# Expert weights loaded in two half-height transfers: a two-layer encoder with a mixture of experts on one core

## The chip, the core and the metric

The program runs on one NeuronCore of a Trainium2 chip. The metric is the device time of one execution in microseconds (us); the time of a kernel is the median of its runs.

## What is computed

The reference is an encoder of two layers on 256 tokens of width 1024, all in float32. Each layer has a mixer (a long convolution and a differential attention) and a feed-forward part. The feed-forward part of layer 0 is dense; that of layer 1 is a mixture of eight experts, of which each token takes two. Cut to what matters here:

```
def swiglu(x, w_gate, w_up, w_down):
    return (jax.nn.silu(x @ w_gate) * (x @ w_up)) @ w_down

def moe_ffn(x, w_router, w_gate, w_up, w_down):
    logits = (xt @ w_router).astype(F32)
    top_val, top_idx = lax.top_k(logits, TOP_K)
    ...
    def run(args):
        xb, e = args
        return swiglu(xb, w_gate[e], w_up[e], w_down[e])
    ...
```

D_MODEL is 1024, D_FF 2752, N_EXPERTS 8, TOP_K 2. The three float32 matrices of one expert are 33.8 MB, and the kernel reads all eight experts.

## The kernel before

All weights are streamed from HBM in slabs. A slab is at most 128 partitions x 2048 float32 (1 MiB, 8 KB in each partition). SyncE issues the loads in the order in which TensorE will use them, and waits before each until its place in SBUF is free. The stages are the mixer of layer 0, the dense feed-forward part, the mixer of layer 1, and the mixture of experts, here the expert stage. In the first three stages the slabs go to six `raw` places, and ScalarE and VectorE split each into two parts (`w_hi`, `w_lo`) for TensorE. These loads are issued by `put` and are of no concern to the change.

In the expert stage TensorE reads the slabs as they land. Eight blocks follow one another, one for each expert. A block has 34 slabs: 33 are loaded by the lines at L792 to L796 (30 of 1 MiB, two of 768 KB, one of 512 KB), and the last, `last_rows`, by four transfers of 16 partitions x 4 KB (L785). The 33 go to the twelve places of `ring`; the first twenty places of the stage also use eight other buffers that have come free by then (`h_slot`, the two halves of `filters`, `xv_slot`, `tmp_dft_slot`, two `gate_slots`, `hT_lo_slot`). So SyncE starts to load the experts while the mixer of layer 1 still runs: six of them (the places of `h`, `filters0`, `filters1`, `xv`, 0 and 1) ahead of the router.

Two things order the loads. `slot_free` makes SyncE wait on `slab_used`, which TensorE counts up after the last matmul that reads a slab. Each place has a semaphore `raw_loaded`, to which a landed transfer adds 16, and TensorE's `loaded` waits for the value that `loaded_by_place` gives. The twelve ring places enter the stage with the count that the `raw` loads left on the first six of them.

On TensorE a block is six chunks of `gate_up_moe` (L2121 in blocks with room for 64 tokens, L2126 with 96) and the `down` steps between them (L2136 and L2143, or L2157). There is also a code path for further blocks, in a hardware loop, for experts with more tokens than their room.

Of the kernel before, what the change touches and what calls it, by code (L numbers as in the profile page):

```python
# [32 lines left out]
P = 128  # L33
# [9 lines left out]
NE, TOPK = 8, 2  # L43
# [3 lines left out]
RAW_SLOTS, SPLIT_SLOTS = 6, 3  # L47
# [25 lines left out]
RING = 2 * RAW_SLOTS  # L73
# [7 lines left out]
MOE_PLACES = MOE_SLABS - 1  # L81
SKIPPED = 3
# [10 lines left out]
PLACE = {("mix", 0): 0, ("ffn", 0): MIX_SLABS, ("mix", 1): MIX_SLABS + FFN_PLACES, ("ffn", 1): 2 * MIX_SLABS + FFN_PLACES}  # L93
# [7 lines left out]
def raw_slot(stage, p):  # L101
    return raw_place(stage, p) % RAW_SLOTS
# [7 lines left out]
def width_of(stage, p):  # L110

    return FFN_WIDTHS[p % FFN_SLABS] if stage[0] == "ffn" else SLAB
# [5 lines left out]
MOE_AT = [P * sum(MOE_WIDTHS[:p]) for p in range(34)] + [3 * FF * D]  # L118
# [15 lines left out]
def slot_of(place):  # L134

    return FIRST_TURN[place] if place < len(FIRST_TURN) else RING_ORDER[(place - len(FIRST_TURN)) % RING]


def loaded_by_place(place):

    slot, turn = slot_of(place), 0 if place < len(FIRST_TURN) else 1 + (place - len(FIRST_TURN)) // RING
    return 16 * (turn + 1) + (16 * (PLACE["ffn", 1] // RAW_SLOTS) if slot in range(RAW_SLOTS) else 0)


def is_late(b, p):
# [4 lines left out]
def moe_place(b, p):  # L150

    return MOE_PLACES * b + p + (SKIPPED if is_late(b, p) else 0)
# [124 lines left out]
def trunk(nc, x_in, slabs, par_d, lamv_d, hid_d, wf3_d, hyb_d, nffn_d, wr_d,  # L277
# [21 lines left out]
    def sem(name):  # L299
        if name not in semaphores:  # L300
            semaphores[name] = ctx.enter_context(nc.semaphore(name))
        return semaphores[name]
# [118 lines left out]
    def bank(step, i):  # L421
        return PS[BANKS[step][i]]
# [9 lines left out]
    def weight(b, p):  # L432

        slot = slot_of(moe_place(b, p))
        return EXTRA_AT[slot] if slot in EXTRA else SLOTS[:, slot, :]
# [44 lines left out]
    def wait_drained(eng, layer, step, i):  # L480

        eng.wait_ge(*drain_of(layer, step, i))
# [235 lines left out]
    def _(sp):  # L718
# [10 lines left out]
        slot = raw_slot(("mix", 0), 0)  # L729
# [5 lines left out]
        for layer in range(DEPTH):  # L735
            stage, first = ("mix", layer), FIRST["mix", layer]
            for p in range(0 if layer else 1, MIX_SLABS - layer):
                slot = raw_slot(stage, p)
                put(slot, RAW[:, slot, :], slabs["mix"][layer, p], raw_place(stage, p))

            if layer == 0:
                for p in (0, 2):
                    slot, at = raw_slot(("ffn", 0), p), slice(SLAB_AT[p], SLAB_AT[p + 2])
                    put(slot, RAW[:, slot, :].rearrange("p (h n) -> p h n", h=2),
                        slabs["dense"][0, at].rearrange("(h p n) -> p h n", h=2, p=P), raw_place(("ffn", 0), p))
                for p in range(4, FFN_SLABS):
                    slot, at, width = raw_slot(("ffn", 0), p), slice(SLAB_AT[p], SLAB_AT[p + 1]), width_of(("ffn", 0), p)
# [4 lines left out]
        def slot_free(b, at, p):  # L752

            place = moe_place(at, p)
            slot = slot_of(place)
            if place >= len(FIRST_TURN):
                blocks, slab = freed_by(at, p)
                sp.wait_ge(slab_used, MOE_SLABS * b + (MOE_SLABS * blocks + slab + 1 + first))
            elif slot == "h":
                wait_filled(sp, 1, "sc3", 1)  # L760
            elif slot in ("filters0", "filters1"):
                sp.wait_ge(event("ys_ready", 1), 2)
            elif slot == "xv":
                wait_filled(sp, 1, "yT", 1)
            elif slot == "tmp_dft":
                sp.wait_ge(event("merged", 1), 4)
            elif slot == "gates0":
                wait_filled(sp, 1, "mTb", 1)
            elif slot == "hT_lo":
                wait_filled(sp, 1, "rt", 1)  # L770
            elif slot in range(RAW_SLOTS):
                sp.wait_ge(lo_ready, slab_at(PLACE["ffn", 1] + slot - RAW_SLOTS) + 1)
            elif slot in range(RING):
                sp.wait_ge(slab_used, first - SPLIT_SLOTS + 1 + (RING_ORDER.index(slot) - RAW_SLOTS) // 2)

        def load_slab(e, b, at, p):

            if p == MOE_SLABS - 1:
                if at == 0:
                    sp.wait_ge(sem("last_rows_zeroed"), 1)  # L780
                else:
                    sp.wait_ge(slab_used, MOE_SLABS * b + first)
                rows = (TAIL - P) // 4
                for q in range(4):
                    sp.dma_start(R["last_rows"][QUARTER * q:QUARTER * q + rows, :],  # L785
                                 slabs["moe"][e, MOE_AT[p] + q * rows * D:MOE_AT[p] + (q + 1) * rows * D]
                                 .rearrange("o (r n) -> (o r) n", n=D)).then_inc(last_rows_loaded, 16)
                return
            to, width = weight(at, p), MOE_WIDTHS[p]
            loaded = raw_loaded[slot_of(moe_place(at, p))]  # L790
            slot_free(b, at, p)
            pieces = 2 if at == NE and p in REJOINED else 1  # L792
            for i in range(pieces):
                cols = slice(i * width // pieces, (i + 1) * width // pieces)
                sp.dma_start(to[:, cols],  # L795
                             slabs["moe"][e, MOE_AT[p]:MOE_AT[p + 1]].rearrange("o (p n) -> p (o n)", p=P)[:, cols]).then_inc(loaded, 16)  # L796

        def load_block(e, b):

# [16 lines left out]
        with sp.If(nb > NE):  # L816
            with sp.Fori(NE, nb) as b:
                e = sp.value_load(R["nbe"][0:1, bass.ds(b, 1)], min_val=0, max_val=NE - 1)
# [917 lines left out]
    def _(pe):  # L1736
# [87 lines left out]
        for layer in range(DEPTH):  # L1824
# [141 lines left out]
            if layer == 1:  # L1966
# [4 lines left out]
                for kd in range(KD):  # L1971
# [6 lines left out]
                    for tb in range(TB):  # L1978
                        tok = slice(tb * P, (tb + 1) * P)
                        both = R["wr_parts"][:, kd, :, :].rearrange("p a e -> p (a e)")  # L1980
                        to = bank("rt", tb)
# [17 lines left out]
            tbs, rows = TB, P  # L1999
# [74 lines left out]
            def pick_tokens(b, room):  # L2074

                pe.wait_ge(psel_ready, b + 1)
                cols = 32 if room == CAP else 64
                for kd in range(KD):
                    for tb in range(TB):
                        for q in range(0, P, cols):  # L2080
                            ins = mm(picked_to(kd)[q:q + cols, 0:room], X[:, tb, kd * P + q:kd * P + q + cols], R["psel"][:, tb, 0:room],
                                     start=tb == 0, stop=tb == TB - 1)
                    if kd % 4 == 3:
                        ins.then_inc(picked, 1)

            def dense_block():

                n0 = first

                def slot(p):  # L2090
                    return (first + p) % SPLIT_SLOTS
                for part in range(4):
                    gate_up(n0 + part, slot(part), 2 * part, 2, CHUNK, 0, 0, "fht")
                    if part == 0:
                        turn_h(0, 2)
                        turn_h(0, 3)
                for c in range(1, NCH + 1):
                    p, parity, width = 3 * c + 1, c % 2, CHUNK if c < NCH else TAIL
                    gate_up(n0 + p, slot(p), 0, 4, width, c, parity)
                    turn_act(c - 1, 1 - parity)  # L2100
                    gate_up(n0 + p + 1, slot(p + 1), 4, 4, width, c, parity)
                    down(n0 + p + 2, slot(p + 2), c - 1, c == 1)
                turn_act(NCH, 0)
                down(n0 + 34, slot(34), NCH, False, tiles=((0, P),))
                down_last(n0 + 35, slot(35), NCH)
# [91 lines left out]
            def turn_spread(b):  # L2197

                pe.wait_ge(sem("spread_ready"), b - (NE - 2))
                rows = CAP if is_heavy(b) else LCAP  # L2200
                for tb in range(TB):
                    ins = nc.tensor.transpose(PS[0][0:rows, tb * P:(tb + 1) * P], R["spread_sum"][:, tb, 0:rows], IDENT[:, :])
                ins.then_inc(sem("spread_turned"), 1)
# [14 lines left out]
            if layer == 0:  # L2218
                dense_block()
            else:  # L2220
                wait_drained(pe, 1, "pos", 0)
                pick_tokens(0, LCAP)
                for b in range(NE - 1):
                    moe_block(b)
                moe_block(NE - 1, None, lambda: turn_spread(NE - 1))
                spread(NE - 1)
                pe.wait_ge(sem("blocks_known"), 1)
                nb = pe.value_load(R["nbi"][0:1, 0:1], min_val=NE, max_val=NBLK)
                with pe.If(nb > NE):
                    with pe.Fori(NE, nb) as b:  # L2230
                        pe.wait_ge(sem("combined"), 4 * b + 4)
                        pick_tokens(b, CAP)
                        turns = pe.snap(16 * ((MOE_PLACES + SKIPPED) // RING) * b - 16 * ((MOE_PLACES + SKIPPED) // RING) * NE)
                        moe_block(b, turns, lambda: turn_spread(b))
                        spread(b)

# [135 lines left out]
```

## Time and profile before

| | us |
|---|---|
| median of 3 runs | 1295.62 (1294.94 to 1297.51) |
| the profiled execution | 1296.07 |
| its span | 1294.3 |
| TensorE busy, matmuls | 1217.1 (94%) |
| VectorE, ScalarE, GpSimd busy | 608.0, 337.8, 45.1 |
| chain that ended last | TensorE 71%, DMA 12%, VectorE 5% of the span |

The span is the time from the first to the last instruction; some 1.8 us of the execution lie outside it. A window of the trace gives, for a stretch, each engine's busy time, the clock that TensorE was granted (1.00 is full), the mean busy share of the core's 16 DMA engines and the bytes that they moved. A packet is put down whole to the moment that it starts, so a share can pass 1 in a short window.

### The profile page before, as it was taken

The page shows a single profiled execution, that of the slowest core. Times are in us where ns is not written, and L with a number is a line of the kernel's source. Part 1 is how long each engine was busy: PE and PEld are TensorE (multiplying, and loading weights), DVE is VectorE, ACT ScalarE, POOL GpSimd, SP SyncE. Part 2 cuts the span into 40 slices and gives each one's busy share as a digit, 9 for nine tenths or more (in the row PEclk, how much of TensorE's full clock was granted, in tenths as well). Part 3 has the DMA queues.
Part 4 walks back from the last instruction along what each step waited for, and adds up shares of the span by engine and source line. Part 5 has one row for each costly group of instructions (what it writes and reads, how often), then busy time and mean ns, then how long its engine had stood idle before and what let it go on. Part 6 is the DMA issues. An engine that isn't in the chain of part 4 may idle for free.

```text
span 1294.3 us, 24431 instructions
## 1 busy us (share of the span) xinstructions
PE 1217.1 (94%) x10627; PEld 775.8 (60%) x10627; DVE 608.0 (47%) x1078; ACT 337.8 (26%) x519; POOL 45.1 (3%) x56
## 2 busy tenths in 40 slices
PE   6999999999999999999999999889999988898966
PEld 5787678888887887778644553245645522454212
DVE  6888987655544988987362113211111032111223
ACT  4444554643443444464300000000000000000000
POOL 0011010100000011010000000000000000000010
PEclk9999999999999999999999999999999999999999
DMA  9434433755543344446799999999999999999994
GB/s 349 154 136 157 163 127 137 273 179 190 187 147 130 135 159 163 163 171 254 330 379 397 420 395 421 420 396 420 389 419 420 388 422 402 403 420 387 421 420 178
DMA packets 55876, 376.13 MB, mean 291 GB/s; under 512 B 6706, under 2 KB 7298, under 8 KB 13780
## 3 DMA queue, kind: packets, MB, share of 16 engines
q1 hardware_dynamic: 54690, 370.17, 72.8%
q0 software_dynamic: 1072, 4.33, 1.1%
q8 instruction: 86, 1.41, 0.4%
q14 instruction: 26, 0.21, 0.1%
q10 hardware_dynamic: 2, 0.00, 0.0%
HBM read 371.07 MB, written 3.41 MB: 289 GB/s over the span
## 4 chain that ended last, share of the span: by engine, by line
PE 71%; DMA 12%; DVE 5%; SPq 2%; issue 1%; ACT 1%; POOL 0%; DVEq 0%; ACTq 0%
PE bank L2126 17%; DMA ring<-in_moe 12%; PE bank L1741 8%; PE bank L1742 8%; PE bank L2136 6%; PE bank L2121 6%; PE bank L2042 4%; PE bank L1791 4%; PE bank L2019 3%; PE bank L2143 3%; PE bank L2157 2%; DVE ys L1196 1%; SPq L795 1%; PE bank L1886 1%; PE bank L1754 1%
## 5 line engine op out<-in xcount | busy, mean ns | idle before, releaser
L2126 PE MATMUL bank<-ring,hT_block 128*32 128x256 f32 (+1 forms) x4608 | 230.3, 357 | 4.9 <-issue 4.7
L1207 DVE TENSOR_TENSOR w_lo<-raw,w_hi 128x2048 fp32r<-128x2048 f32 (+2 forms) x92 | 201.4, 2201 | 52.5 <-ACT w_hi L907 52.3
L1741 PE MATMUL bank<-w_hi,hT_hi 128*128 128x512 f32 (+1 forms) x528 | 209.3, 396 | 2.4 <-DVE hT_lo L1196 1.6
L1615 DVE TENSOR_TENSOR act_moe<-silu_moe,bank 128x256 f32<-128x256 f32 (+1 forms) x40 | 19.5, 488 | 398.4 <-ACT silu_moe L1141 398.4
L1742 PE MATMUL bank<-w_hi,hT_lo 128*128 128x512 f32 (+1 forms) x528 | 205.1, 388 | 0.0
L2126 PEld LDWEIGHTS bank<-ring,hT_block 128*32 128x32 f32 x4608 | 143.7, 110 | 95.8 <-issue 14.2
L907 ACT ACTIVATE w_hi<-raw 128x2048 fp32r<-128x2048 f32 (+2 forms) x92 | 169.1, 1848 | 88.5 <-PE bank L1791 42.7
L2121 PE MATMUL bank<-ring,hT_block 128*64 128x512 f32 (+1 forms) x704 | 144.4, 550 | 22.8 <-DMA ring<-in_moe 22.8
L1141 ACT ACTIVATE silu_moe<-bank 128x256 f32<-128x256 f32 (+3 forms) x48 | 19.7, 410 | 544.6 <-PE bank L2126 303.6
L2121 PEld LDWEIGHTS bank<-ring,hT_block 128*64 128x64 f32 x704 | 47.9, 136 | 119.4 <-issue 64.7
L1741 PEld LDWEIGHTS bank<-w_hi,hT_hi 128*128 128x128 f32 x528 | 99.2, 188 | 24.9 <-issue 4.5
L1742 PEld LDWEIGHTS bank<-w_hi,hT_lo 128*128 128x128 f32 x528 | 99.2, 188 | 20.2 <-issue 1.0
L2157 PE MATMUL bank<-ring,act_T 128*64 128x512 f32 x336 | 80.9, 610 | 19.8 <-DMA ring<-in_moe 19.2
L2136 PE MATMUL bank<-ring,act_T 128*32 128x512 f32 x672 | 90.2, 593 | 1.2 <-issue 1.2
L1791 PE MATMUL bank<-w_lo,hT_hi 128*128 128x512 f32 x352 | 87.9, 392 | 0.5 <-DVE w_lo L1207 0.3
L1791 PEld LDWEIGHTS bank<-w_lo,hT_hi 128*128 128x128 f32 x352 | 65.5, 188 | 15.5 <-DVE w_lo L1207 1.7
L2157 PEld LDWEIGHTS bank<-ring,act_T 128*64 128x64 f32 x336 | 23.4, 138 | 71.1 <-issue 51.5
L2143 PE MATMUL bank<-ring,act_T 128*32 128x512 f32 x336 | 50.6, 592 | 0.0
L1623 DVE STREAM_TRANSPOSE act_T<-act_moe 32x128 f32<-32x128 f32 x160 | 48.4, 303 | 2.6
L2136 PEld LDWEIGHTS bank<-ring,act_T 128*32 128x32 f32 x672 | 25.5, 110 | 40.0 <-issue 36.9
L1741 PE MATMUL bank<-hT_hi,w_hi 128*128 128x256 f32 x192 | 47.1, 286 | 0.0
L1742 PE MATMUL bank<-hT_lo,w_hi 128*128 128x256 f32 x192 | 46.5, 283 | 0.0
(282 smaller groups left out, 1200.7 us busy)
## 6 DMA issues: line engine op xcount, KB each, us to landing
ring<-in_moe SPq DMA_DIRECT2D x232, 1024.0 KB, 23.4
raw<-in_mix SPq DMA_DIRECT2D x56, 1024.0 KB, 4.8
raw<-in_dense SPq DMA_DIRECT2D x30, 1024.0 KB, 4.7
ring<-in_moe SPq DMA_DIRECT2D x16, 768.0 KB, 26.1
ring<-in_moe SPq DMA_DIRECT2D x8, 512.0 KB, 24.0
filters<-in_moe SPq DMA_DIRECT2D x2, 1024.0 KB, 9.9
gate_slots<-in_moe SPq DMA_DIRECT2D x2, 1024.0 KB, 11.0
last_rows<-in_moe SPq DMA_DIRECT2D x32, 64.0 KB, 15.2
```

Of the source, the lines that this page charges most:

```text
L907: nc.scalar.activation(HI[:, split_slot, 0:width], RAW[:, raw_slot, half:half + width], ACT.Copy)\
L1207: vec.tensor_tensor(LO[:, split_slot, 0:width], RAW[:, raw_slot, half:half + width], HI[:, split_slot, 0:width].bitcast(F32), ALU.subtract ...
L1623: ins = vec.transpose(R["act_T"][to:to + QUARTER, c % 2, 0:tiles, QUARTER * t:QUARTER * t + QUARTER], act_tile(c)[frm:frm + QUARTER, i * t ...
L1741: mm(out_, left[0], right[0], start=start, stop=False)
L1742: mm(out_, left[1], right[1], start=False, stop=False)
L1791: ins = mm(bank(step, tb)[:, :], HTH[:, kd, tok], w_lo, start=False, stop=sp_)
L2042: ins = mm(PS[4 + 2 * tb + half][0:rows, :], left[0:h, k, tok], right[0:h, s, at:at + 512], start=first and k == 0, stop=last and k == 1)
L2121: ins = mm(x_banks(c)[64 * half:64 * half + 64, 0, 0:2 * width], tokens[:, kd, 0:LCAP], at[:, (4 * k + 2 * half) * width:(4 * k + 2 * half ...
L2126: ins = mm(x_banks(c)[QUARTER * q:QUARTER * q + QUARTER, t, 0:width], tokens[:, kd, QUARTER * t:QUARTER * t + QUARTER], at[:, (4 * k + q) ...
L2136: ins = mm(Y_BANKS[half][q:q + 32, :], left[:, k, 32 * t:32 * t + 32], rights[k][:, half * 512:half * 512 + 512], start=start and k == 0, ...
L2143: ins = mm(Y_BANKS[1 - k][q:q + 32, :], left[:, k, 64:96], rights[k][:, half * 512:half * 512 + 512], start=start, stop=stop)
L2157: ins = mm(Y_BANKS[half][64 * half:64 * half + 64, :], left[:, k, 0:LCAP], rights[k][:, half * 512:half * 512 + 512], start=start and k == ...
```

## The change

Each of the 33 large loads of a block is issued as two transfers, one that writes partitions 0 to 63 and one that writes partitions 64 to 127, each of the full width of the slab. Both add 16 to the same semaphore, so the value that TensorE waits for rises by 32 for each use of a place. `last_rows`, the results that go out to `slot_y`, and the loads of the other stages are as before.

```diff
@@ def loaded_by_place(place):
-    return 16 * (turn + 1) + (16 * (PLACE["ffn", 1] // RAW_SLOTS) if slot in range(RAW_SLOTS) else 0)
+    return 32 * (turn + 1) + (16 * (PLACE["ffn", 1] // RAW_SLOTS) if slot in range(RAW_SLOTS) else 0)
@@ def load_slab(e, b, at, p):
             for i in range(pieces):
                 cols = slice(i * width // pieces, (i + 1) * width // pieces)
-                sp.dma_start(to[:, cols],
-                             slabs["moe"][e, MOE_AT[p]:MOE_AT[p + 1]].rearrange("o (p n) -> p (o n)", p=P)[:, cols]).then_inc(loaded, 16)
+                for rows in (slice(0, P // 2), slice(P // 2, P)):
+                    sp.dma_start(to[rows, cols],
+                                 slabs["moe"][e, MOE_AT[p]:MOE_AT[p + 1]].rearrange("o (p n) -> p (o n)", p=P)[rows, cols]).then_inc(loaded, 16)
@@ the loop of further blocks, on TensorE
-                        turns = pe.snap(16 * ((MOE_PLACES + SKIPPED) // RING) * b - 16 * ((MOE_PLACES + SKIPPED) // RING) * NE)
+                        turns = pe.snap(32 * ((MOE_PLACES + SKIPPED) // RING) * b - 32 * ((MOE_PLACES + SKIPPED) // RING) * NE)
```

This is what SyncE issues before, from the first expert slab to the end of the first block (`raw<-in_mix` is the mixer's last slab):

```order
L795 DMA h_slot<-in_moe 128x2048
L795 DMA filters<-in_moe 128x2048 x2
L795 DMA xv_slot<-in_moe 128x2048
L723 DMA raw<-in_mix 128x2048
L795 DMA ring<-in_moe 128x2048 x2
L795 DMA tmp_dft_slot<-in_moe 128x2048
L795 DMA ring<-in_moe 128x2048 x4
L795 DMA gate_slots<-in_moe 128x2048 x2
L795 DMA ring<-in_moe 128x2048 x6
L795 DMA hT_lo_slot<-in_moe 128x2048
```

And the same place in the changed kernel:

```order
L796 DMA h_slot<-in_moe 64x2048 x2
L796 DMA filters<-in_moe 64x2048 x4
L796 DMA xv_slot<-in_moe 64x2048 x2
L723 DMA raw<-in_mix 128x2048
L796 DMA ring<-in_moe 64x2048 x4
L796 DMA tmp_dft_slot<-in_moe 64x2048 x2
L796 DMA ring<-in_moe 64x2048 x8
L796 DMA gate_slots<-in_moe 64x2048 x4
L796 DMA ring<-in_moe 64x2048 x12
L796 DMA hT_lo_slot<-in_moe 64x2048 x2
```

The order of the slabs is the same; each stands there as two neighbours with half the partitions. From the second block on the expert's number is read at run time, and before each transfer stands one more instruction (ISA). This is SyncE at the start of the second block, in the changed kernel:

```order
L785 DMA last_rows<-in_moe 16x1024 x4
L814 TENSOR_LOAD nbe
L814 ISA x2
L796 ISA
L796 DMA ring<-in_moe 64x2048
L796 ISA
L796 DMA ring<-in_moe 64x2048
```

Before, an ISA and one transfer of 128x2048 stood there for each slab; now there are two such pairs. The other engines' instructions are the same, but for the values that TensorE waits for.

## Rows read from the trace of the kernel before

**Rows 1.** The page: GB/s moved, in 40 slices of the span.

```profile
GB/s 349 154 136 157 163 127 137 273 179 190 187 147 130 135 159 163 163 171 254 330 379 397 420 395 421 420 396 420 389 419 420 388 422 402 403 420 387 421 420 178
```

**Rows 2.** Windows of the expert stage: window, us, engines' busy time, PEclk, DMA share, GB/s.

```profile
604.00:622.00 18.00, 18.00 (x89) 15.12 (x88) 8.86 (x11) 7.93 (x14) 0.95 (x1) 1.00 0.96 389
622.00:640.00 18.00, 16.69 (x153) 13.62 (x153) 7.61 (x33) 6.81 (x16) 1.31 (x4) 1.00 1.01 422
640.00:647.00 7.00, 7.00 (x35) 2.77 (x32) 1.26 (x4) 0.38 (x1) 0.00 (x0) 1.00 0.04 16
647.00:1272.00 625.00, 577.14 (x7390) 268.97 (x7388) 128.66 (x409) 32.49 (x85) 3.92 (x4) 1.00 1.01 406
```

**Rows 3.** Waits of TensorE after 640 us: total us, times, longest.

```profile
PE bank L2121 <- DMA ring<-in_moe: 22.8, 31, 1.8
PE bank L2157 <- DMA ring<-in_moe: 19.2, 21, 2.2
```

**Rows 4.** DMA issues of the page: count, KB each, median us from issue to landing.

```profile
ring<-in_moe SPq DMA_DIRECT2D x232, 1024.0 KB, 23.4
...
last_rows<-in_moe SPq DMA_DIRECT2D x32, 64.0 KB, 15.2
```

**Rows 5.** Timeline of SyncE's queue, 570 to 604 us: start, us, what was issued.

```profile
570.70 0.43 SPq L795 DMA_DIRECT2D h_slot<-in_moe  x1
...
581.58 0.33 SPq L723 DMA_DIRECT2D raw<-in_mix  x1
583.89 4.92 SPq L795 DMA_DIRECT2D ring<-in_moe  x2
603.70 0.33 SPq L795 DMA_DIRECT2D tmp_dft_slot<-in_moe  x1
```

**Rows 6.** Timeline of SyncE's queue at the start: a load of 64 partitions x 8 KB.

```profile
2.89 0.48 SPq L707 DMA_DIRECT2D wf<-in_wf  x1
```

**Rows 7.** Windows while that load ran.

```profile
6.50:7.00 0.50, 0.50 (x2) 0.22 (x2) 0.00 (x0) 0.50 (x3) 0.00 (x0) 1.00 0.92 197
7.00:7.50 0.50, 0.50 (x2) 0.00 (x0) 0.00 (x0) 0.50 (x3) 0.00 (x0) 1.00 0.94 197
7.50:8.00 0.50, 0.05 (x1) 0.00 (x0) 0.32 (x1) 0.50 (x3) 0.00 (x0) 1.00 1.04 213
8.00:8.50 0.50, 0.00 (x0) 0.00 (x0) 0.47 (x2) 0.48 (x3) 0.11 (x1) 1.00 1.14 238
```

**Rows 8.** Issues of 512 KB in the DMA list: `raw` 128 partitions, `wf` 64 partitions.

```profile
raw<-in_dense SPq DMA_DIRECT2D x1, 512.0 KB, 3.1
wf<-in_wf POOLq DMA_DIRECT2D x1, 512.0 KB, 4.7
```

**Rows 9.** Windows in which the first four `last_rows` transfers ran.

```profile
680.00:681.00 1.00, 1.00 (x8) 0.32 (x6) 0.00 (x0) 0.00 (x0) 0.00 (x0) 1.00 1.09 246
681.00:682.00 1.00, 1.00 (x8) 0.40 (x6) 0.00 (x0) 0.00 (x0) 0.00 (x0) 1.00 0.80 115
682.00:683.00 1.00, 1.00 (x6) 0.29 (x4) 0.00 (x0) 0.00 (x0) 0.00 (x0) 1.00 0.88 205
```

**Rows 10.** Windows at the end of the stream.

```profile
1264.00:1265.00 1.00, 0.87 (x6) 0.00 (x0) 0.00 (x0) 0.00 (x0) 0.00 (x0) 1.00 1.04 430
1272.00:1273.00 1.00, 1.00 (x6) 0.17 (x4) 0.90 (x2) 0.00 (x0) 0.00 (x0) 1.00 0.45 188
1280.00:1281.00 1.00, 0.99 (x6) 0.42 (x8) 0.00 (x0) 0.00 (x0) 0.00 (x0) 1.00 0.12 49
```

**Rows 11.** The chain that ended last, after 1255 us: start, us, what.

```profile
1253.74 26.23 DMA ring<-in_moe
```

**Rows 12.** ScalarE's splits of the mixer's last slabs, 575 to 640 us.

```profile
L907 ACT ACTIVATE w_hi<-raw x6: 1915/1920/1922, 579.6 to 607.4; 128x2048 fp32r<-128x2048 f32 x6
```

**Rows 13.** Windows with a granted clock under 1.00.

```profile
852.00:854.00 2.00, 2.00 (x8) 0.38 (x6) 0.00 (x0) 0.00 (x0) 0.00 (x0) 0.50 0.97 397
854.00:856.00 2.00, 2.00 (x12) 0.47 (x12) 0.02 (x1) 0.03 (x1) 0.00 (x0) 0.93 1.06 442
```

## The prediction

> **What bounds the kernel now.** I read the page's row of rates first. Up to about 600 us the DMA engines move 127 to 330 GB/s after the first slice; from there to the end it is 387 to 422 [rows 1]. So the only part that the change touches is also the only one in which memory traffic is dense. The windows of that stage show both sides nearly full: from 647 to 1272 us TensorE is busy 577 of 625 us, and the 16 DMA engines have a busy share of 1.01 at 406 GB/s; the best stretch, 622 to 640 us, has 422 [rows 2], which I take as the full rate. The waits tell which of the two leads. TensorE stood still for transfers 22.8 and 19.2 us in blocks with room for 64 tokens [rows 3], and in the others hardly at all. A slab lands 23.4 us after its issue [rows 4]; at 422 GB/s 1 MiB takes 2.48 us, so some nine slabs are queued. The stage is balanced, and has nothing with which to pay for a slower stream: nearly all that the transfers lose, the end loses.
>
> **The change part by part.** The bytes are the same. Of 264 large loads, six are issued before 603.70 us [rows 5], while there is slack; the other 258 (234 of 1 MiB, 16 of 768 KB, 8 of 512 KB) are 250 MiB, 262.1 MB, and from 603.70 us the queue is never empty in the changed kernel if it slows down.
>
> *Issuing.* 258 more issues. One takes 0.33 to 0.43 us of SyncE's queue [rows 5], 0.48 at the start [rows 6]. Two per slab are under 1 us, against 2.48 us for moving it: hidden, cost 0. Uncovered, it would be 258 x 0.43 = 111 us, but the nine slabs in the queue cover it. TensorE's waits keep their number and place.
>
> *Moving half a slab.* The trace before has no stream of 64-partition loads, but it has one such load: `wf`, 64 partitions x 8 KB, the packet size of the slabs, issued at 2.89 us behind others [rows 6]. While it ran, 6.5 to 8.5 us, the engines moved 197, 197, 213 and 238 GB/s, 211 on average, at a busy share of about 1 [rows 7]. The reader is to see the two columns together: all 16 engines are at work, and they move half of what they move for 128 partitions. So it isn't that half of the engines do the work; each works at half speed, as two of them would that write through one entry to SBUF. Its second copy, on GpSimd's queue, agrees: 4.7 us to landing against 3.1 for 512 KB over 128 partitions [rows 8], though others ran beside it.
>
> *Two neighbours in the queue.* Do an upper and a lower half fill each other's gap? The four `last_rows` loads are the nearest row: 16 partitions each, two in the lower half and two in the upper, issued in a row. In 680 to 683 us the engines moved 246, 115 and 205 GB/s at shares of 0.80 to 1.09 [rows 9]: 0.57 MB where 1.27 would pass, so 1.66 us lost, and 2.3 us for four loads that need 0.62 at the full rate. They ran nearly one after another, each at its own narrow rate. If the halves do the same, the rate is 211.
>
> The Trainium skill speaks against this change too: SBUF — State Buffer, section "Can I just issue two DMAs to hit both halves?", answers no, with 6% gained by two concurrent transfers at partitions 0 and 64 over one; its section on the port swizzle has 196 GB/s for partitions 0 to 63 at 1 MiB. By the page the rate would be 208 GB/s, and the sum below 1920 us as an estimate. The trace's 211 agrees with the 196; that neighbours don't help, rows 9 show for narrow loads only.
>
> *What speaks for more than 211.* The 16 engines don't march in step for long. All loads had been issued when, at 1264 us, the share was 1.04; it was 0.45 at 1272 and still 0.12 at 1280 [rows 10], so the first and the last engine finish some 16 us apart. Half a slab at the full rate takes 1.24 us. Two engines that share an entry and are a whole half-slab apart don't meet at all: one is in the lower half while the other is in the upper. If such distances are spread evenly, half of the bytes meet and half do not, and the rate is 2 / (1/211 + 1/422) = 281 GB/s. The stream starts in step, though (the queue runs dry before 603.70), engines that both wait for one entry can't drift apart by their own speed, and a slab counts as landed only when the slowest pair has it. I choose a point a quarter of the way from 211 to 281 in time per byte: 1 / (0.75/211 + 0.25/281) = 225 GB/s. This is the number of the prediction with the least behind it; both ends stay in the range.
>
> *The sum.* Start of the dense stream 603.7. The halves: 262.1 MB / 225 = 1165. `last_rows` 8 x 2.3 = 18. The results to `slot_y`, seven blocks, 2.4 MB at the full rate: 6. The lag of the last engine, 16. From the last landing (1253.74 + 26.23 = 1280.0 [rows 11]) to the end of the span 14.3. Together 1823 us of span; with the 1.8 outside it 1825, and the profiled execution lies 0.45 over the median, which changes nothing here. The same sum with 422 GB/s and the 7 us of an empty queue at 640 [rows 2] gives 1288 for the kernel before, 8 short of its 1296; the rest is that the fast engines waited and TensorE held the ring. The added semaphore writes I set at 0.
>
> *What waits ahead.* The mixer's last slab is issued behind four expert slabs, at 581.58 us [rows 5]. These end at about 570.7 + 4.2 MB / 225 = 589, and it lands near 593. ScalarE starts its last split at 607.4 us [rows 12], so 14 us cover it. The six slabs before the router land by 604 plus a few us, TensorE begins the experts at about 640; from place 12 or so it waits for each slab, about 4.7 us apart, of which it computes 2.5.
>
> **The rivals.**
>
> *The halves stay in step throughout:* 211 GB/s, 262.1 / 211 = 1242, end at 1902 us. For it: rows 7 and 9, both of short stretches. Against it: rows 10. Chance 0.20.
>
> *The engines drift apart further than I think:* 281 to 400 GB/s, 933 to 655 us in place of 1165, end between 1593 and 1315. For it rows 10. Against it that contention itself holds them together. Chance 0.15.
>
> *Nothing happens:* each pair settles a half-slab apart and stays there, since nothing then disturbs it; or the entry isn't what limits `wf`. The rate is 422 as before, TensorE and the waits are the same, 1296 us. Rows 9 speak against it, in their short stretch. Chance 0.12.
>
> *Faster:* the same full rate, and in addition the work of a slow entry is shared between two engines, which takes away up to half of the 16 us by which the last engine lags: 1288 us. It decides only if the rate stays above some 415 GB/s. Nothing in the rows shows what slows an engine. Chance 0.05.
>
> *TensorE's clock falls:* with 577 us of work in some 1200 it idles half of the time. At a granted 0.50 (1.2 GHz of 2.4) it started 8 matmuls in 2 us where it started 12 in the next 2 us, at 0.93 [rows 13]. All its expert work at the lower level would be about 1154 us, nearly the stream's own time, and what doesn't overlap comes on top: 1940 to 2000 us. Against it: through 48 us of short idle times between 647 and 1272 us the mean clock stayed at 1.00 [rows 2]. Chance 0.06.
>
> **How the numbers follow.** My forecast, a rate between 213 and 281 GB/s, ends between 1593 and 1892 us: chance 0.42, the value 1825. With steps of 0.20, 0.15, 0.12, 0.05 and 0.06 for the others that makes 1. The range goes from 1400 (a rate of 354) to 1940: it leaves out no change and faster, the smaller part of the further drift, and the upper part of the clock's case, together about 2 in 10. The likeliest case's own range is 1593 to 1902. Slower by over 0.2%, which is about what a measurement of this kernel can tell from no change: 0.20 + 0.15 + 0.42 + 0.06 = 0.83. Same 0.12, faster 0.05.
>
> **What would show it.** In windows after 650 us a DMA share of about 1 at 210 to 280 GB/s; if the share is 1 and the rate 420, the halves do not meet. If the share is near 0.5, the halves are served by half of the engines each, and my reading of rows 7 is wrong. TensorE's waits for `ring` should sum to some 500 to 600 us, in both kinds of block; SyncE should wait for free places as before, since the ring is still full of loads under way. If the rate rises from block to block, the engines drift apart; if it is flat at 211, they don't. If the rows before 570 us differ, something other than the halves has changed. The number would be wrong most easily by my quarter of the way: each 10 GB/s there is about 50 us.

## The result, and the profile after

| | before | changed |
|---|---|---|
| median, us | 1295.28 (1293.46 to 1297.51) | 1641.61 (1621.79 to 1647.79) |
| profiled execution, us | 1296.07 | 1635.77 |
| span, us | 1294.3 | 1633.9 |

The change makes the kernel slower by a quarter: the ratio of the times is 1.257, 95% interval 1.248 to 1.267. This ratio is taken from the two faster of the four executions; the ratio of the medians is 1.267. The change also makes the time less steady: its four executions lie within 1.6% of one another, where those of the kernel before lie within 0.3%.

These are windows of the changed kernel, with the columns of [rows 2].

```profile
604.00:622.00 18.00, 18.00 (x89) 15.09 (x88) 8.85 (x11) 7.92 (x14) 0.95 (x1) 1.00 1.02 219
650.00:750.00 100.00, 66.50 (x502) 24.31 (x502) 23.67 (x107) 3.41 (x10) 0.00 (x0) 0.90 1.02 230
850.00:950.00 100.00, 59.59 (x464) 17.91 (x464) 13.69 (x41) 2.62 (x6) 0.00 (x0) 0.95 1.02 270
950.00:1050.00 100.00, 68.10 (x856) 30.09 (x860) 13.30 (x43) 3.62 (x10) 0.00 (x0) 0.98 1.02 285
1150.00:1250.00 100.00, 69.61 (x1107) 32.93 (x1103) 6.91 (x19) 2.89 (x8) 0.00 (x0) 0.97 1.02 260
1250.00:1350.00 100.00, 63.17 (x424) 19.41 (x413) 16.75 (x52) 4.04 (x11) 0.00 (x0) 0.96 1.02 295
647.00:1612.00 965.00, 652.26 (x7390) 263.10 (x7388) 129.88 (x409) 32.41 (x85) 3.93 (x4) 0.95 1.01 270
```

Read the last two columns together, as in [rows 7]. The 16 DMA engines are busy all the time (1.02), at 219 GB/s when the dense stream begins, where [rows 2] had 389 and 422. Then the rate climbs, to 230, 270 and 285, falls back to 260, and comes to 295. TensorE is busy 652 of 965 us.

The trace also holds the time of each packet, which no view prints. In 622 to 640 us, 923 of 925 packets of 8 KB took under 350 ns in the kernel before (median 309). In the changed kernel each of the 484 took 525 ns or more, with a median of 612: every packet takes twice as long. In 950 to 1050 us the median is 461 ns; 260 of 3145 took under 350, and 2314 took 350 to 550.

The waits of TensorE after 640 us, which answer to [rows 3]:

```profile
PE bank L2122 <- DMA ring<-in_moe: 119.4, 70, 4.0
PE bank L2127 <- DMA ring<-in_moe: 89.7, 83, 2.4
PE bank L2158 <- DMA ring<-in_moe: 50.2, 27, 3.1
PE bank L2137 <- DMA ring<-in_moe: 34.6, 26, 3.2
```

Now both kinds of block wait, 294 us in these four groups. The issue row that answers to [rows 4]:

```profile
ring<-in_moe SPq DMA_DIRECT2D x464, 512.0 KB, 31.9
```

And the end of the chain, which answers to [rows 11]:

```profile
1589.41 30.55 DMA ring<-in_moe
...
1620.01 1.94 PE bank L2158 x8
```

The last landing is at 1619.96 us, and 13.9 us follow it, as 14.3 did before.

### The profile page after: what moved, and what is told of

It is laid out like the page before. It is cut to its first block, busy times and chain, and to the rows that moved or that the text cites. A ratio compares the mean times of both kernels' runs of the same rounds, so it can differ in the third digit from the quotient of the medians.

```text
span 1633.9 us, 25157 instructions
## 1 busy us (share of the span) xinstructions
PE 1292.8 (79%) x10627; PEld 770.7 (47%) x10627; DVE 607.8 (37%) x1078; ACT 337.8 (21%) x519; POOL 45.0 (3%) x56
## 4 chain that ended last, share of the span: by engine, by line
SPq 42%; PE 29%; DMA 14%; issue 4%; DVE 4%; ACT 0%; POOL 0%; DVEq 0%; ACTq 0%
SPq L796 39%; DMA ring<-in_moe 10%; PE bank L1742 7%; PE bank L1743 6%; PE bank L2043 4%; PE bank L1792 3%; DMA hT_lo_slot<-in_moe 3%; PE bank L2020 2%; DMA last_rows<-in_moe 2%; SPq L785 1%; SPq L805 1%; DVE ys L1197 1%; PE bank L1887 1%; PE bank L1755 1%; PE bank L1787 1%
## 5 line engine op out<-in xcount | busy, mean ns | idle before, releaser
L2127 PE MATMUL bank<-ring,hT_block 128*32 128x256 f32 (+1 forms) x4608 | 245.3, 362 | 98.7 <-DMA ring<-in_moe 89.7
L2122 PE MATMUL bank<-ring,hT_block 128*64 128x512 f32 (+1 forms) x704 | 168.0, 606 | 119.7 <-DMA ring<-in_moe 119.4
L2127 PEld LDWEIGHTS bank<-ring,hT_block 128*32 128x32 f32 x4608 | 136.9, 111 | 217.0 <-DMA ring<-in_moe 132.6
L2158 PE MATMUL bank<-ring,act_T 128*64 128x512 f32 x336 | 96.0, 700 | 54.4 <-DMA ring<-in_moe 50.2
## 6 DMA issues: line engine op xcount, KB each, us to landing
ring<-in_moe SPq DMA_DIRECT2D x464, 512.0 KB, 31.9
```

Source lines behind the costliest of these rows:

```text
L2122: ins = mm(x_banks(c)[64 * half:64 * half + 64, 0, 0:2 * width], tokens[:, kd, 0:LCAP], at[:, (4 * k + 2 * half) * width:(4 * k + 2 * half ...
L2127: ins = mm(x_banks(c)[QUARTER * q:QUARTER * q + QUARTER, t, 0:width], tokens[:, kd, QUARTER * t:QUARTER * t + QUARTER], at[:, (4 * k + q) ...
L2158: ins = mm(Y_BANKS[half][64 * half:64 * half + 64, :], left[:, k, 0:LCAP], rights[k][:, half * 512:half * 512 + 512], start=start and k == ...
```

## The experiments

Theory A is the prediction's: a transfer that writes only partitions 0 to 63, or only 64 to 127, reaches half of the entries to SBUF, so that the 16 engines, all at work, share them; the cost falls as the engines drift apart (the distances between them in the stream change). The first rival is that the number or the size of the transfers costs. All edits but that of `e11_one_last` are made to the changed kernel. Medians of 4 or more runs unless said otherwise; the kernel before, beside them on the same chip, had 1294.6 to 1295.6 us.

| run | edit | us |
|---|---|---|
| e1_columns | halves by columns | 1310.60 |
| e12_even_odd | even and odd partitions | 1295.56 |
| e4_turned | lower, upper, upper, lower | 1787.47 |
| e7_quads | quarters, lower and upper by turns | 1632.80 |
| e8_quads_grouped | quarters, two lower, two upper | 1715.45 |
| e2_lead4, e3_lead8 | 4 or 8 small transfers on an empty queue | 1643.28, 1652.68 |
| e5_mid4, e6_mid8 | 4 or 8 small transfers, 8 rows, in a full queue | 1618.98, 1639.55 |
| e9_engines4 | 4 small transfers, 4 rows | 1650.53 |
| e10_engine1 | 4 small transfers, 1 row | 1610.18 (one run) |
| e11_one_last | kernel before, last rows in one wide transfer | 1284.42 |

### Is it the number of transfers?

```diff
-                for rows in (slice(0, P // 2), slice(P // 2, P)):
-                    sp.dma_start(to[rows, cols],
...
+                for j in range(2):
+                    cols = slice((2 * i + j) * width // (2 * pieces), (2 * i + j + 1) * width // (2 * pieces))
+                    sp.dma_start(to[:, cols],
...
```

> Each slab goes as two transfers again, but cut by columns: all 128 partitions and half of the row (4 KB in place of 8 KB) in each. Number of transfers, semaphore values and bytes are those of the changed kernel. Theory A (a 64-partition transfer reaches only half of the entries to SBUF, two engines at each): full rate, 405 to 422 GB/s in the expert stage, 1290 to 1305 us. Theory B (twice as many transfers in the queue are what costs: SyncE's issues fill 39% of the chain of the changed kernel): the rate stays at 220 to 300 GB/s and the time at 1600 to 1660 us.

1310.60 us, a ratio to the kernel before of 1.012 (1.011 to 1.014), and some 6 us above the expected range. Two windows:

```profile
622.00:640.00 18.00, 16.70 (x152) 13.76 (x152) 7.61 (x33) 6.80 (x16) 1.31 (x4) 1.00 1.03 409
1050.00:1150.00 100.00, 83.53 (x822) 32.92 (x822) 23.47 (x77) 4.77 (x13) 0.00 (x0) 1.00 1.02 400
```

409 GB/s where [rows 2] has 422, at a full share: the engines are as busy and move 3% less, which goes with the 4 KB packets. The same number of transfers with shorter packets thus costs 16 of the 346 us. The number costs nothing, as the run with even and odd partitions shows.

### Is it 64 partitions, or one side of SBUF?

```diff
-                for rows in (slice(0, P // 2), slice(P // 2, P)):
+                for rows in (slice(0, P, 2), slice(1, P, 2)):
```

> The changed kernel with the two transfers of a slab taken as the even and the odd partitions, in place of the lower and the upper half. Both are 64 partitions with 8 KB each, and each reaches both halves of SBUF. Theory A as it first stood (what counts is how many of the entries to SBUF a transfer reaches as a whole): full rate, 1290 to 1315 us. Theory A as the small transfers have left it (what counts is which engines are at the same entry at the same time, with groups of engines that share entries): each engine now writes two packets to one half and two to the other; engines in step still meet, but half the distance parts them: the stream starts at 220 to 300 GB/s and climbs faster than in the changed kernel, 1400 to 1600 us. Rival (64 partitions in a transfer cost the same wherever they are): 1610 to 1660 us.

1295.56 us over ten runs; the ratio to the kernel before is 1.0007 (0.9998 to 1.0017), no change. Three windows:

```profile
605.00:622.00 17.00, 17.00 (x85) 14.22 (x84) 8.76 (x11) 7.71 (x13) 0.95 (x1) 1.00 0.92 370
622.00:640.00 18.00, 16.70 (x152) 14.11 (x152) 7.71 (x34) 7.02 (x18) 1.31 (x4) 1.00 1.01 422
647.00:1272.00 625.00, 581.56 (x7408) 273.07 (x7406) 131.03 (x413) 32.42 (x85) 3.93 (x4) 0.99 1.01 406
```

The last two are the rates of [rows 2], 422 and 406. Of its packets of 8 KB in 622 to 640 us, 921 of 925 took under 350 ns. It has the number of transfers, packets of 8 KB, semaphores and issues of the changed kernel, so the whole loss hangs on which 64 partitions a transfer holds. Theory A as it first stood forecast this; my amended form, in which even and odd partitions would still meet, did not. But the first form, which counts the entries of one transfer alone, says nothing of the climb and of the effect of order that follow.

One thing moves with the partitions in every edit here: the rows in HBM that the transfer reads. No run separates the two. Against HBM as the cause speaks only this: the small transfers further down read rows of the first expert slab and write nothing to SBUF, and nearly all their packets took 309 to 312 ns in the midst of halves whose packets took some 600.

### Does the cost depend on how long an engine stays on one side?

```diff
@@ e4_turned
-                for rows in (slice(0, P // 2), slice(P // 2, P)):
+                for rows in ((slice(0, P // 2), slice(P // 2, P)), (slice(P // 2, P), slice(0, P // 2)))[moe_place(at, p) % 2]:
```

> The changed kernel with the order of the two halves turned in every second slab: lower, upper, upper, lower. Each engine then stays in the same half of SBUF for two transfers in a row. Theory A with drift: the engines of a pair must be twice as far apart to miss each other, so the rate climbs later from 211 to 220 GB/s and the time is longer than 1642, by some 30 to 120 us. Rival (the cost is per transfer, or on the side of HBM): no difference, 1620 to 1650 us.

1787.47 us (1758.87 to 1799.12), 146 more than the changed kernel: the sign as expected, the size above the 30 to 120. Its fastest execution is 111 us above the slowest of the changed kernel. Its windows:

```profile
650.00:750.00 100.00, 68.00 (x428) 23.33 (x428) 24.25 (x109) 3.41 (x10) 0.00 (x0) 0.83 1.02 217
1250.00:1350.00 100.00, 64.82 (x1011) 32.07 (x1004) 4.94 (x12) 2.69 (x8) 0.00 (x0) 0.97 1.02 232
1650.00:1750.00 100.00, 59.24 (x194) 14.07 (x193) 20.83 (x55) 1.92 (x5) 3.92 (x4) 0.83 1.00 275
```

The rate climbs here too, but at 1250 us it is 232 where the changed kernel has 295. Bytes, transfers and packets are the same; only the order differs, and with it an engine's stay on a side, which is twice as long.

The second pair of kernels cuts each half by columns too, and differs in order alone (semaphores count 64 per slab):

```diff
@@ e7_quads
-                for rows in (slice(0, P // 2), slice(P // 2, P)):
+                for rows, part in ((lower, 0), (upper, 0), (lower, 1), (upper, 1)):
+                    cols = slice((2 * i + part) * width // (2 * pieces), (2 * i + part + 1) * width // (2 * pieces))
@@ e8_quads_grouped
+                for rows, part in ((lower, 0), (lower, 1), (upper, 0), (upper, 1)):
```

> Each slab goes as four transfers of 64 partitions and half of the columns (4 KB rows), in the order lower, upper, lower, upper. Semaphore values are 64 per slab. An engine now stays in one half of SBUF for 16 KB, half as long as in the changed kernel. Theory A with drift: half the distance is enough to miss each other, so the rate leaves 211 to 220 GB/s sooner: 1540 to 1620 us (the 4 KB packets cost some 1.2% of the rate, as the columns run showed). Rival (cost by number of transfers or by packet): well above 1650.

> The same four transfers per slab in the order lower, lower, upper, upper. Number, size and packets are those of the run before; only the order differs. An engine stays in one half of SBUF for 32 KB, as in the changed kernel. Theory A with drift: 1620 to 1680 us, and 50 to 120 us above the alternating order. Rival (number and size of transfers alone matter): the same time as the alternating order.

1632.80 (1620.70 to 1643.07) and 1715.45 us (1659.49 to 1769.00): 83 us apart by their medians, inside the 50 to 120, though each is above its own range, by 13 and 35 us. The executions of the grouped order scatter over 110 us. The fastest of them is 16 us above the slowest with alternating order, so the sign is sure and the size is not. One window of each, from the slowest execution of each, first the alternating order:

```profile
950.00:1050.00 100.00, 67.67 (x716) 26.84 (x710) 11.83 (x39) 2.63 (x7) 0.00 (x0) 0.91 1.04 261
```

and the grouped one:

```profile
950.00:1050.00 100.00, 59.67 (x448) 20.80 (x452) 10.26 (x35) 2.65 (x8) 0.00 (x0) 0.85 1.04 228
```

Two pairs of kernels that differ in order alone say the same: a shorter stay on one side costs less. It is what drifting engines would give, but the stay isn't all. The grouped order has the stay of the changed kernel, 32 KB, and is 74 us slower by the medians. The alternating order has half of it and is only 9 us faster. Cutting finer cost 16 us where all 128 partitions were written; here it seems to cost more, and no run shows why.

### Can the engines be set apart by hand?

Small transfers from HBM to an unused HBM buffer, ahead of the seventh slab (e2, e3) or the fifteenth (the others), were to hold back some engines:

```diff
+        def lead():
+
+            for i in range(LEAD):
+                rows = slabs["moe"][0, 0:P * SLAB].rearrange("(p n) -> p n", p=P)[0:32:4, :]
+                sp.dma_start(aside[:, 2 * i * SLAB:(2 * i + 1) * SLAB], rows).then_inc(sem("led"), 16)
...
+            if at == 0 and p == 6:
+                lead()
```

`e5_mid4` and `e6_mid8` have `p == 14`; `e9_engines4` has rows `[0:16:4, :]`, `e10_engine1` the one row `[0:1, 0:SLAB - 1]`.

> The changed kernel with four small transfers ahead of the dense stream (before the seventh expert slab): 8 rows of 8 KB each, from HBM to an unused HBM buffer, which should occupy eight of the sixteen DMA engines for four packets, as long as half a slab takes at the full rate. Theory A with drift (two engines share an entry only while both are in the same half, and start in step): the pairs now start half a slab apart, so the stream starts at 380 to 420 GB/s where the changed kernel has 218 to 230, and falls as the engines drift; if they keep their distance the time is near 1300, if they lose it within some hundred us 1450 to 1600. Rival (the half rate has nothing to do with when the engines meet): 218 to 230 GB/s at first, 1620 to 1650 us.

> The same with eight of the small transfers, so that the distance is two half-slabs: both engines of a pair are in the same half again. Theory A with drift: 215 to 240 GB/s at first, as in the changed kernel, 1600 to 1650 us. If the small transfers help by something else than the distance, this kernel gains as much as the one with four.

1643.28 us (1589.14 to 1685.21) and 1652.68 (1640.83 to 1690.84). The first had 227 GB/s in 605 to 622 us, where theory A wanted 380 to 420, so both came out as the rival said. They are weak evidence, though: the queue was empty, SyncE issued the small transfers 0.67 us apart while one packet takes 0.31, and the first half-slab was issued when they were done.

> The changed kernel with four small transfers of 8 rows x 8 KB (HBM to an unused HBM buffer) ahead of the fifteenth expert slab. Ahead of the seventh slab the queue was empty, so that SyncE's own issue times spaced the small transfers out and eight engines were not held back behind the others. Here some ten transfers stand in the queue, and the four are worked off back to back. Theory A with drift: from the moment they are worked off (about 640 to 670 us) the pairs are half a slab apart, and the rate in the windows of 10 us behind it rises from 220 to 350 to 420 GB/s, and falls back in the next hundred us or so as the engines drift; the total is 20 to 200 us below 1642. Rival (the distance within a pair doesn't matter, or the pairs are not one of the first eight engines with one of the last eight): 220 to 230 GB/s as in the changed kernel.

> The same place with eight small transfers: the distance is two half-slabs and the engines of a pair are in the same half again. Theory A with drift: 210 to 240 GB/s behind them, apart from the some 3 us in which the small transfers themselves run, and a total of 1610 to 1660 us. If it rises as in the run with four, it isn't the distance.

1618.98 us (1612.16 to 1647.78) and 1639.55 (1613.73 to 1660.55). The windows of the second, before, during and after its small transfers:

```profile
635.00:645.00 10.00, 8.99 (x98) 4.90 (x98) 0.86 (x4) 1.60 (x6) 0.00 (x0) 1.00 1.03 227
645.00:655.00 10.00, 10.00 (x48) 4.00 (x46) 7.97 (x35) 0.77 (x2) 0.00 (x0) 1.00 1.01 251
655.00:665.00 10.00, 10.00 (x50) 4.05 (x48) 5.56 (x26) 0.38 (x1) 0.00 (x0) 1.00 1.00 224
```

The small transfers are 0.52 MB, which alone would add 52 GB/s to a window of 10 us; it rose by 24. So the halves lost 28, about what eight engines lose at half rate (113 GB/s) in 2.5 us, and the other eight didn't speed up in the meantime. The packets bear this out: in 645 to 650 us 64 took under 400 ns, as many as the small transfers have, and of the others ten took 400 to 450 and the rest more. In 650 to 700 us the rate is 230 GB/s with four of them and 225 with eight, where the changed kernel has 227. I expected 350 or more with four: a clear miss.

> As the run with four small transfers ahead of the fifteenth slab, but each of 4 rows, which should occupy four engines. With eight engines held back nothing followed: while the small transfers ran, the packets of the halves on the other engines still took over 450 ns each, so both engines of a pair were held back, or neither. If the pairs are four engines apart, holding back four of them parts four of the eight pairs: behind the small transfers 4 of 8 pairs run at the full rate, 220 goes to about 330 GB/s, and falls back as they drift. If the pairs are neighbours, or two apart, or if distance within a pair is no matter: 220 to 230 GB/s as before.

> Four small transfers of one row of 2047 floats, which should occupy a single engine for 1.2 us; whichever its partner is, they are then half a slab apart. Theory A: one pair of eight goes from half to the full rate, 220 to some 245 GB/s in the windows behind the small transfers (650 to 700 us), where the changed kernel has 222 to 231; one packet in five or so takes 309 to 330 ns, where the changed kernel has none under 400 ns at that time. Rival (the distance within a pair doesn't matter): no packets at the full rate, 222 to 231 GB/s.

1650.53 us (1610.95 to 1709.01) with four rows, and 1610.18 in one run with one. In 650 to 700 us the first has 231 GB/s. The second, and then the changed kernel, in the same window:

```profile
650.00:700.00 50.00, 40.39 (x276) 14.50 (x272) 18.66 (x91) 2.18 (x7) 0.00 (x0) 0.90 1.02 238
```

```profile
650.00:700.00 50.00, 38.21 (x270) 13.80 (x268) 18.00 (x88) 2.19 (x7) 0.00 (x0) 0.90 1.02 227
```

11 GB/s more, of which 5 were there before the small transfers (225 against 220 in 635 to 645 us), where one freed pair of eight should give about 25. I had also expected one packet in five to take 309 to 330 ns; of the 1449 of this window none took under 450. While the four rows were moved and right behind them (645 to 650 us), one packet of a half took 309 ns and each of the others over 450. The picture of fixed pairs, parted by one half-slab, is not borne out by any of these runs.

Later these kernels do differ from the changed one:

```profile
850.00:950.00 100.00, 71.83 (x419) 20.54 (x413) 18.90 (x59) 4.14 (x11) 0.00 (x0) 0.90 1.02 331
850.00:950.00 100.00, 67.05 (x400) 20.20 (x392) 21.03 (x68) 4.38 (x12) 0.00 (x0) 0.94 1.02 335
```

That is 331 and 335 GB/s, first with four rows and then with one, and 316 in `e5_mid4`, where the changed kernel has 270. In 1450 to 1550 us the three have 250, 235 and 237, where it has 286. These are single traces, of the fastest or the only execution of each of the three, and executions of one kernel differ by 26 us and more. They show that the rate wanders both ways, and not whether the small transfers had a part in it.

### A faster kernel

If narrow loads cost by the entries that they reach, the kernel before has its own: the four `last_rows` transfers. This edit is made to the kernel before; the added rows are zeros, stored with the weights.

```diff
-                for q in range(4):
-                    sp.dma_start(R["last_rows"][QUARTER * q:QUARTER * q + rows, :],
-                                 slabs["moe"][e, MOE_AT[p] + q * rows * D:MOE_AT[p] + (q + 1) * rows * D]
-                                 .rearrange("o (r n) -> (o r) n", n=D)).then_inc(last_rows_loaded, 16)
+                sp.dma_start(R["last_rows"][:, :],
+                             slabs["moe"][e, MOE_AT[p]:MOE_AT[p + 1]].rearrange("o (p n) -> p (o n)", p=P)).then_inc(last_rows_loaded, 16)
```

> The kernel before, with its only narrow loads of the expert stage made wide: the four transfers of 16 partitions x 4 KB for the last rows of each expert become one of 128 partitions x 4 KB, whose other rows are zeros stored with the weights (twice the bytes, 512 KB). By the row of the kernel before the four cost 2.3 us of the stream per block, one wide load would take 1.24: 1 us less in each of eight blocks. Theory A (narrow loads cost by the entries that they reach, and the stage is limited by transfers as much as by TensorE): 1288 to 1293 us against 1295. Rival (TensorE's own work sets the end of each block): no change within 0.2%.

1284.42 us (1284.14 to 1285.29), a ratio to the kernel before of 0.992 (0.991 to 0.993): 10 us or 0.8% faster, with 2 MB more to move, and some 4 us below the expected 1288 to 1293. A window of it:

```profile
1050.00:1150.00 100.00, 90.25 (x1092) 40.12 (x1092) 17.89 (x57) 4.50 (x12) 0.00 (x0) 1.00 1.01 420
```

and the same of the kernel before:

```profile
1050.00:1150.00 100.00, 85.62 (x978) 36.72 (x978) 20.36 (x68) 4.50 (x12) 0.00 (x0) 1.00 1.01 410
```

The gain is more than the 8 us that I worked out, and shows that transfers, not TensorE alone, set the pace of the kernel before. The edit also makes one transfer of four small ones; how much is due to the width and how much to the number, it does not show.

## Why the prediction came out as it did

*The first half of the mechanism was right.* The stream begins at 219 GB/s at a full share, against the 211 read from `wf`, and its packets take twice the time of those before; the even and odd partitions show that it hangs on which 64 partitions a transfer holds, and not on the number of transfers. The second half, that two engines at one entry halve each other's rate and are free when a half-slab apart, is not shown. Taking one engine away for four packets freed no other, and most packets of the later stages are neither near 309 ns nor near 612.

*The term that was mis-sized is the rate.* The chosen 225 GB/s gave 1165 us for the halves. Measured: from 603.5 us to the last landing at 1620.0 are 1016 us; less 18 for `last_rows`, 6 for the results and 16 for the lag, as in the sum, 976 remain, a rate of 262.1 / 976 = 269 GB/s. In time per byte that is 86% of the way from 211 to 281, where I went 25%. The 189 us in this term are the whole error: the profiled execution, the shortest but one, took 1636 us against 1825. My argument was that engines at one entry can't drift apart by their own speed, so that the rate stays near its start. It did not: 230, 251, 270, 285 GB/s in successive windows of 100 us from 650 us on. Also, single windows reach 295, above the 281 of evenly spread distances, so that figure was no ceiling either. The total fell inside my forecast of 213 to 281 GB/s (by the sum 213 ends at 1890 us, not at 1892), but that the mean came so near to 281 has no worked-out cause behind it.

*The other terms held.* The tail after the last landing, 13.9 against 14.3 us. The lag of the last engine, by the fall of the share at the end of the stream, was set at 16 us:

```profile
1598.00:1600.00 2.00, 1.49 (x8) 0.29 (x4) 0.00 (x0) 0.00 (x0) 0.00 (x0) 1.00 0.96 217
1610.00:1612.00 2.00, 1.26 (x8) 0.46 (x8) 0.97 (x1) 0.00 (x0) 0.00 (x0) 1.00 0.61 206
1620.00:1622.00 2.00, 1.99 (x9) 0.61 (x10) 0.00 (x0) 0.00 (x0) 0.00 (x0) 1.00 0.04 16
```

some 20 us. More issues cost nothing, as the even and odd partitions show. Nothing waited at the start of the stage: the dense stream begins at 603.48 us, as before. TensorE's waits for `ring` are 294 us and not 500 to 600; most of that follows from the rate. One sign was wrong: SyncE was to wait for free places as before. After 640 us its longest such waits, first before and then in the changed kernel, are

```profile
SPq L795 <- PE bank L2126: 119.5, 70, 4.8
SPq L796 <- PE bank L2122: 20.7, 9, 10.7
```

The places were nearly always free when SyncE came to them; what took its time is in the last section.

*The rivals.* Staying in step at 211 (1902 us) is out, though the kernel with turned halves comes near it for most of its length. No change and faster are out. Further drift, 281 to 400 GB/s, was the nearest: the measured 269 lies between my choice and its edge. TensorE's clock fell more often, to a mean of 0.95 in 647 to 1612 us, but TensorE idles 313 us there, and I see no us at the end that it cost; this wasn't tried by itself.

*The rule of the Trainium skill* (SBUF — State Buffer, "Can I just issue two DMAs to hit both halves?") had the sign. The 208 GB/s estimated from it is near the rate of the first 36 us (219 to 221); over the stage the measured 269 decides. In the same place the Trainium skill says that only one transfer spanning all 128 partitions reaches all ports. Even and odd partitions, 64 each, ran at the full rate, and here the measurement decides; by the Trainium skill's own table of ports (SBUF — State Buffer, "Door 1: The DMA port swizzle") even partitions reach all 16.

*What stays open:* which engines share an entry, and what parts them. That the rate depends on the order of the halves is shown. That it depends on the stay through engines drifting apart is only argued: setting them apart by hand has failed, the rate falls as well as climbs, and finer cuts with the same stay were slower. Whether the limit lies at the entries to SBUF or at the rows read from HBM is argued too.

## What to carry to other kernels

Before you cut a transfer by partitions, look at which partitions each piece holds: in a stage limited by transfers, 0 to 63 and 64 to 127 cost 26% of the time, even and odd cost nothing, and columns cost 1.2% by their shorter packets. Read the DMA share and the GB/s together: a full share at half the usual rate was here the mark of such transfers. One such load elsewhere in the trace (`wf`) gave the rate at which the stream would begin, 211 for 219 GB/s, before the change was made; it did not give the mean of a long stream, 269. And look for small, narrow loads in the kernel that you have; one wide load, padded with zeros, in place of four gave the only gain here, 0.8%.

## What the runs showed of the hardware that was not expected

Four executions of the changed kernel differ by 26 us, and five of the kernel with four rows held back by 98, where 13 of the kernel before, on one chip, lie within 3.1. So the rate of half-sided transfers depends on something that the program doesn't set; what it is, these runs don't show.

SyncE's queue became a place of its own on the chain. This is the page's row of the changed kernel, share of the span by engine:

```profile
SPq 42%; PE 29%; DMA 14%; issue 4%; DVE 4%; ACT 0%; POOL 0%; DVEq 0%; ACTq 0%
```

and this that of the kernel with even and odd partitions:

```profile
PE 67%; SPq 10%; DMA 7%; DVE 4%; issue 2%; ACT 1%; POOL 0%; DVEq 0%; ACTq 0%
```

In the changed kernel a half lands 31.9 us after its issue and takes 0.524 MB / 269 = 1.95 us to move, so some 16 stand in the queue (an estimate), and SyncE spends its time in issuing instead of in waiting for free places. Since the share stayed full, and the other kernel lost nothing with the same issues, this did not set the time.
